# Softmax weights divided ahead of the turn, values as transposed rows, the mask on GpSimd, and logits over parts of the columns

## The reference

```python
def forgetting_attention(q, k, v, f, ...):          # 6 heads of 64, blocks of 128 query rows
    c = cumsum(log_sigmoid(f + f_bias))
    s = (q_block @ k[:hi].T) * scale + c[lo:hi, None] - c[None, :hi]
    s = where(k_pos <= q_pos, s, -inf)
    out = softmax(s) @ v[:hi]
def hybrid_mixer(h, ...):
    return concatenate([o_dn, o_fx, o_pl]) @ w_out    # gated DeltaNet 384, attention 384, pooling 256
def moe_swiglu(h, router, w_gate, w_up, w_down):      # 8 experts, 1536 wide, top 2
    probs = softmax(h @ router); gates = top 2 of probs, normalised
    out = sum over e of gates[:, e] * ((silu(h @ w_gate[e]) * (h @ w_up[e])) @ w_down[e])
```

## Time and profile before

| | |
|---|---|
| median of 3 runs | 1545.66 us (1545.61 to 1547.28) |
| profiled execution | 1552.2 us |
| span of its instructions | 1550.3 us |
| TensorE busy | 1518.6 us (98%) |
| VectorE busy | 1186.3 us (77%) |
| ScalarE busy | 1015.9 us (66%) |
| GpSimd busy | 70.1 us (5%) |
| mean granted TensorE clock | 0.993 of full |

### The profile page before, as it was taken

One profiled execution on the slowest core, in us unless ns is written; L12 is line 12 of the kernel. 1 busy time (PEld: TensorE's weight loads), 2 busy tenths in 40 slices (PEclk: granted clock), 3 DMA queues, 4 the chain that ended last, 5 costly groups with the idle time before them and its releaser, 6 DMA issues.

```text
span 1550.3 us, 27067 instructions
## 1 busy us (share of the span) xinstructions
PE 1518.6 (98%) x9990; PEld 1303.5 (84%) x9990; DVE 1186.3 (77%) x1485; ACT 1015.9 (66%) x1433; POOL 70.1 (5%) x92
## 2 busy tenths in 40 slices
PE   9999999999999999999999999999999999999998
PEld 7988888878878888899788888998788888888886
DVE  6677877775678877787776556886688888888887
ACT  6666656565566656696564445875467777777775
POOL 0000000000000000031000000120000000000000
PEclk9999999999999999999999999999899999999999
DMA  7544554544525555464154555461699999999995
GB/s 282 185 144 170 190 189 186 190 151 175 190 82 176 204 189 189 141 196 161 58 211 184 202 189 181 149 185 42 244 366 358 408 382 381 384 403 388 371 362 220
DMA packets 54795, 351.09 MB, mean 226 GB/s; under 512 B 6208, under 2 KB 9968, under 8 KB 14896
## 3 DMA queue, kind: packets, MB, share of 16 engines
q1 hardware_dynamic: 46512, 330.94, 57.2%
q0 software_dynamic: 8192, 18.90, 4.7%
HBM read 341.90 MB, written 7.91 MB: 226 GB/s over the span
## 4 chain that ended last, share of the span: by engine, by line
PE 90%; DVE 4%; ACT 3%; issue 1%; DMA 0%; POOL 0%; DVEq 0%; ACTq 0%; SPq 0%; POOLq 0%
PE PS L966 21%; PE PS L1920 16%; PE PS L2053 14%; PE PS L2089 11%; PE PS L1938 8%; PE PS L2054 8%; PE PS L1536 1%; DVE EWL L3850 1%; PE PS L2024 1%; PE PS L1901 1%; ACT MWH L2312 1%; DVE MWL L3174 1%; PE PS L1132 1%; PE PS L1038 1%; PE PS L2114 0%
## 5 line engine op out<-in xcount | busy, mean ns | idle before, releaser
L3850 DVE TENSOR_TENSOR EWL<-W,EWH 128x2048 fp32r<-128x2048 f32 x144 | 329.2, 2292 | 41.6 <-ACT EWH L2867 40.4
L2053 PE MATMUL PS<-HTB,WH 128*128 128x512 f32 x944 | 329.9, 393 | 0.0
L2867 ACT ACTIVATE EWH<-W 128x2048 fp32r<-128x2048 f32 x144 | 276.9, 1923 | 56.5 <-PE PS L1938 30.4
L2054 PE MATMUL PS<-HTB,WL 128*128 128x256 f32 x1008 | 282.5, 280 | 0.0
L3166 DVE TENSOR_TENSOR WL<-W,WH 128x2048 fp32r<-128x2048 f32 x99 | 226.5, 2288 | 35.2 <-ACT WH L2288 32.1
L2288 ACT ACTIVATE WH<-W 128x2048 fp32r<-128x2048 f32 x99 | 189.2, 1917 | 97.8 <-PE PS L2054 86.9
L966 PE MATMUL PS<-MWH,HTB 128*128 128x256 f32 (+1 forms) x940 | 240.5, 341 | 2.4 <-issue 1.5
L3174 DVE TENSOR_TENSOR MWL<-W,MWH 128x1024 fp32r<-128x1024 f32 x136 | 166.6, 1238 | 70.3 <-ACT MWH L2312 67.7
L2053 PEld LDWEIGHTS PS<-HTB,WH 128*128 128x128 f32 x944 | 177.2, 188 | 40.5
L2312 ACT ACTIVATE MWH<-W 128x1024 fp32r<-128x1024 f32 x136 | 142.3, 1055 | 83.2 <-PE PS L966 76.0
L2054 PEld LDWEIGHTS PS<-HTB,WL 128*128 128x128 f32 x1008 | 189.6, 188 | 1.0
(11 more groups left out here) (425 smaller groups left out, 2445.5 us busy)
## 6 DMA issues: line engine op xcount, KB each, us to landing
W<-in_weights SPq DMA_DIRECT2D x311, 1024.0 KB, 5.5
CS<-in_consts POOLq DMA_DIRECT2D x4, 403.5 KB, 4.8
ARENA<-rows_m POOLq DMA_DIRECT2D x8, 192.0 KB, 7.2
ARENA<-rows_m POOLq DMA_DIRECT2D x2, 768.0 KB, 12.5
moe_acc<-X POOLq DMA_DIRECT2D x3, 512.0 KB, 12.3
moe_rows<-HN POOLq DMA_DIRECT2D x3, 512.0 KB, 12.3
X<-in_x SPq DMA_DIRECT2D x2, 512.0 KB, 4.3
W<-in_weights SPq DMA_DIRECT2D x2, 512.0 KB, 6.3
```

Source lines behind the costliest of these rows:

```text
L2053: mm(PS[b][:, :], WH[:, sl, o:o + P], HTB[:, :, kk, :], start=(kk == 0), stop=False, skip_group_check=True)
L2054: ins = mm(PS[b][:, 0:256], WL[:, sl, o:o + P], HTH[:, kk, :], start=False, stop=(kk == KC - 1), skip_group_check=True)
L2867: A(EWH[tile % SPLIT][:, :], tile_ap(w0 + tile), ACT.Copy).then_inc(sem("moe_hi"), 1)
L3850: TT(EWL[tile % SPLIT][:, :], tile_ap(w0 + tile), EWH[tile % SPLIT][:, :].bitcast(F32), SUB).then_inc(sem("moe_lo"), 1)
```

## The change

- **Mask.** ScalarE's copy L2757 goes. GpSimd writes MB with two additions, mask plus row term, as soon as the bank of the turned rows is free, ahead of its accumulating DMAs.
- **Softmax.** One `tensor_tensor_reduce` per row tile adds scores and MB, negates, and reduces; ScalarE's exponential takes scale -1. The bank is given back after the reduction. The new `fx_divided(h)` on VectorE takes reciprocals and scales the exponentials, and `fx_turn` waits for it. `fx_turn(0)` comes after `fx_scores(1)`, and the banks are planned anew.
- **Values.** `fx_values` has FV as weights and PT moving, two heads in the two column halves, and so writes channels by rows. `fx_out` (ScalarE) and `fx_out_lo` (VectorE) write them to HTH and HTL. The division at the end and one of two groups of six transposes, with their splits, go. The output projection's chunk order becomes 6, 7, 3, 4, 5, 2, 0, 1, and `chunk_read(1, 1)` follows chunk 6.
- **Logits.** The router's matrix (padded to 32 columns) is the weight operand, in four column groups with HT moving; ScalarE copies the parts and two matmuls with a picking matrix add them up. Its preparation moves from the start of the kernel to the dilated mixer.
- **Router and start of the MoE.** `kept_at_work` issues matmuls whose result is not used, four ahead of the placing and one behind it. The last norm's scaling is split, so that the second tile's halves (`last_scaled`) lie beside the placing. The selection for experts 1 to 7 and `gates` come after the first gate product, `stage` is split around a weight tile, and `slots_turned` and `turn_selection(3)` move one group of columns later.

```diff
-M2_OUT_CHUNKS = (6, 7, 4, 5, 3, 2, 0, 1)
+M2_OUT_CHUNKS = (6, 7, 3, 4, 5, 2, 0, 1)
...
-            pool.wait_ge(sem(m + "_gd"), 3)
+            await_free_of(pool, (m, "rowT"))
+            for t, sl in enumerate((slice(0, P), slice(P, 384))):
+                w = sl.stop - sl.start
+                pool.tensor_tensor(m2.MB[:, :, sl], bc(cst("cmask")[:, sl], 1, 6), bc(st_gc[:, t, 1, :], 2, w), ADD).then_inc(sem("masks_written"), 1)
+            pool.wait_ge(sem("masks_written"), 2 if m == "m0" else 4)
...
+            def logit_parts():
+
+                key = ("router", "parts")
+                claim(pe, key)
+                for b in range(4):
+                    await_free_of(pe, ("norm", 7, b))
+                for r in range(2):
+                    for j in range(4):
+                        out = bank(key)[32 * j:32 * j + 32, 0:S]
+                        ins = mm(out, st_rt[:, 4 * r + j, :], HT[:, 4 * r + j, :], start=(r == 0), stop=(r == 1), skip_group_check=True)
+                done(ins, key)
+
+            def logits():
+
+                key = ("router", "logits")
+                claim(pe, key)
+                await_free_of(pe, ("router", "parts"))
+                for t in range(NT):
+                    ins = mm(bank(key)[:, t * 8:(t + 1) * 8], mo.PARTS[:, t * P:(t + 1) * P], st_pick, start=(t == 0), stop=(t == NT - 1),
+                             skip_group_check=True)
+                done(ins, key)
 
             turned(0)
             turned(1)
-            claim(pe, ("router", "logits"))
-            logits(0)
-            done(logits(1), ("router", "logits"))
+            logit_parts()
+            logits()
+
+        def kept_at_work(n):
+
+            for k in range(n):
+                mm(PS[3][:, 0:256], ident, X[:, 0, 0:256], start=True, stop=True, skip_group_check=True)
...
-                    pe.wait_ge(sem(m + "f_e"), h + 1)
+                    pe.wait_ge(sem("fx_divided"), 6 * l + h + 1)
...
             def fx_values(g):
 
-                for h in (2 * g, 2 * g + 1):
-                    await_free_of(pe, (m + "f", "t", h))
-                    for n in range(NT):
-                        key = (m + "f", "o", n)
-                        if h == 0:
-                            claim(pe, key)
-                        for kt in range(n + 1):
-                            b = n + kt
-                            ins = mm(bank(key)[:, h * 64:(h + 1) * 64], m2.PT[:, h % 2, b * P:(b + 1) * P], m2.FV[:, kt, h * 64:(h + 1) * 64],
-                                     start=(kt == 0), stop=(kt == n))
-                        if h == FX_H - 1:
-                            done(ins, key)
+                key = (m + "f", "o", g)
+                claim(pe, key)
+                for r in range(2):
+                    await_free_of(pe, (m + "f", "t", 2 * g + r))
+                for kt in range(NT):
+                    for r in range(2):
+                        h = 2 * g + r
+                        ins = mm(bank(key)[half[r], kt * P:256], m2.FV[:, kt, h * 64:(h + 1) * 64], m2.PT[:, h % 2, kt * 256:256 + kt * P],
+                                 start=(kt == 0), stop=(kt == NT - 1), skip_group_check=True)
+                done(ins, key)
...
-            fx_turn(0)
             pe.wait_ge(sem("m2_qd"), l + 1)
             state_out(1)
             fx_scores(1)
+            fx_turn(0)
...
-            for n in range(NT):
-                await_free_of(pe, (m + "f", "o", n))
+            await_free_of(pe, (m, "pz"))
+            await_free_of(pe, (m + "f", "o", 0))
+            await_free_of(pe, (m + "f", "o", 1))
+            m2_chunk(6, first=True)
+            chunk_read(1, 1)
+            m2_chunk(7)
+            m2_chunk(3)
+            m2_chunk(4)
+            for t in range(NT):
+                await_free_of(pe, (m, "o", t))
             for j in range(2):
                 transposed(m, j, M2_OT[j])
-            chunk_read(1, 1)
-            await_free_of(pe, (m, "pz"))
-            m2_chunk(6, first=True)
-            m2_chunk(7)
+            await_free_of(pe, (m + "f", "o", 2))
+            m2_chunk(5)
             for j in range(2):
-                await_free_of(pe, (m, "oT", j))
-            m2_chunk(4)
-            m2_chunk(5)
-            for t in range(NT):
-                await_free_of(pe, (m, "o", t))
-            for j in range(2, 4):
-                transposed(m, j, M2_OT[j])
-            m2_chunk(3)
-            for j in range(2, 4):
                 await_free_of(pe, (m, "oT", j))
             m2_chunk(2)
...
+            kept_at_work(4)
...
-                pe.wait_ge(sem("hn"), 2 * NT * 8)
                 for c in range(KC):
+                    if c % 4 == 0:
+                        pe.wait_ge(sem("hn"), 2 * NT * 8 - (0 if c else 1))
...
-                if not p and gs == 0:
+                if not p and gs == 1:

...
+            release(A(mo.PARTS, bank(key)[:, 0:S], ACT.Copy), key)
...
-                        ins = A(m2.EX[:, h % 2, sl], m2.SM[:, h % 2, sl], ACT.Exp, bias=st_mx[:, j:j + 1], accum_out=st_sum[:, j:j + 1])
+                        ins = A(m2.EX[:, h % 2, sl], m2.SM[:, h % 2, sl], ACT.Exp, scale=-1.0, bias=st_mx[:, j:j + 1], accum_out=st_sum[:, j:j + 1])
...
+            def fx_out(g):
+
+                key = (m + "f", "o", g)
+                await_full(act, key)
+                out_hi(A(HTH[:, 3 + g, :], bank(key)[:, 0:256], ACT.Copy))
...
-            A(m2.MB, bc(cst("cmask"), 1, 6), ACT.Copy).then_inc(sem(m + "_gd"), 1)
...
+            TT(st_rt[:, :, 0:N_EXP], v3(prm("router"), KC), bc(prm("norm")[:, 7 * KC:8 * KC], 2, N_EXP), MUL)
+            dve.tensor_reduce(st_pick, ident.rearrange("p (j e) -> p e j", j=4)[:, 0:N_EXP, :], AX.X, ADD)
...
-                    ins = STT(m2.SM[:, h % 2, sl], bank(key)[:, sl], st_gc[:, n, 1, h:h + 1], m2.MB[:, h, sl], ADD, ADD)
-                release(ins, key)
-                await_free_of(dve, key)
+                    ins = dve.tensor_tensor_reduce(m2.SM[:, h % 2, sl], bank(key)[:, sl], m2.MB[:, h, sl], -1.0, -NEG, ADD, MIN,
+                                                   st_mx[:, 2 * h + n:2 * h + n + 1])
+                ins.then_inc(sem(m + "f_mx"), 1)
+                dve.wait_ge(sem(m + "f_mx"), h + 1)
+                dve.sem_inc(free[uses[key][0]], 1)
+
+            def fx_divided(h):
+
+                dve.wait_ge(sem(m + "f_e"), h + 1)
+                link(dve.reciprocal(st_ri[:, 2 * h:2 * h + 2], st_sum[:, 2 * h:2 * h + 2]))
                 for n, sl in enumerate((slice(0, P), slice(P, 384))):
-                    ins = dve.tensor_reduce(st_mx[:, 2 * h + n:2 * h + n + 1], m2.SM[:, h % 2, sl], AX.X, MAX, negate=True)
-                ins.then_inc(sem(m + "f_mx"), 1)
+                    at = m2.EX[:, h % 2, sl]
+                    ins = TS(at, at, st_ri[:, 2 * h + n:2 * h + n + 1], None, MUL)
+                ins.then_inc(sem("fx_divided"), 1)
+
+            def fx_out_lo(g):
+
+                key = (m + "f", "o", g)
+                await_out_hi()
+                release(TT(HTL[:, 3 + g, :], bank(key)[:, 0:256], HTH[:, 3 + g, :].bitcast(F32), SUB), key)
...
+            last_scaled(1, 0)
             key = ("router", "place")
             await_full(dve, key)
             link(TT(mo.POS, mo.POS, bank(key)[:, 0:16], ADD))
             select(mo.SEL, slice(0, 1))
+            last_scaled(1, 1)
             link(dve.tensor_reduce(mo.MOST, bank(key)[:, 16:24], AX.X, MAX))
             release(TS(MORE[0:1, :], mo.MOST[0:1, :], P + 0.5, None, ALU.is_gt), key)
             await_free_of(dve, key)
             dve.sem_inc(sem("more"), 1)
-            select(mo.SEL, slice(1, N_EXP))
...
+                if not p and gs == 0:
+                    select(mo.SEL, slice(1, N_EXP))
+                    gates()
```

More of the change, by code:

```diff
@@ L428, in plan_m2 @@
         pair("w")
-        for n in range(NT):
-            plan((m + "f", "o", n), 2 + n)
+        for g in range(2):
+            plan((m + "f", "o", g), 2 + g)
         for t in range(NT):
@@ L446, in plan_m2 @@
         rot((m, "vp", 3))
+        rot((m + "f", "o", 2))
         rot = Rot([6, 7])
-        for j in range(4):
+        for j in range(2):
             rot((m, "oT", j))
@@ L501, in build @@
         elif st[0] == "router":
+            plan(("router", "parts"), 6)
             plan(("router", "logits"), 4)
@@ L2280, in hi @@
                 if prev_mixer[name] != "od":
[L2281 removed]
+                    await_full(act, (prev_mixer[name], "oT", 3 if prev_mixer[name] == "ev" else len(M2_OT) - 1))
                 elif j == 0:
@@ L2827, in mixer2 @@
             out_square(0)
+            fx_out(0)
             fx_exp(2)
+            fx_out(1)
             fx_turned(2)
-            for j in range(2):
-                m2_out_T(m, j)
+            fx_out(2)
+            out_root(0)
             out_square(1)
-            out_root(0)
             fd(27)
@@ L3111, in last_norm, with last_scaled @@
             dve.wait_ge(s_late, 16 * (LATE + 1))
```

(25 more changed lines are left out.)

44 lines of the change are left out of this document (19 added, 25 removed).

## The result

Seven executions of the changed kernel took 1551.72 us in the median (1550.32 to 1554.51), seven of the kernel before 1546.79 (1545.61 to 1547.58). The ratio is 1.0033, with a 95% interval from 1.0023 to 1.0043: slower by some 5 us, where 1543.8 had been forecast. The profiled executions say the opposite: 1550.32 us after, 1552.2 before. Which of the two is right, and why they differ, is the first thing to settle.

What follows compares the result with a forecast made beforehand. TensorE, busy 1518.6 of 1550.3 us, was taken as the bound. Mask +7.4, attention -3.2, router -1.8 and second mixer's clock -4.25 sum to -1.85 us on the median 1545.66: 1543.8 us, range 1535.5 to 1552.5.

Steps and rivals of the forecast that it cites:

- part 4: Second mixer's attention: its half-clock stretch disappears as waits go and work gets denser; 4.25 us gained.
- part 2: Attention: less TensorE work and old waits gone, against a new wait for the division; 1.6 us gained per mixer, 3.2 both.
- part 3: Router and MoE start: TensorE 3.4 us earlier at its first expert, but VectorE sets the pace; 1.8 us gained.
- part 1: Mask on GpSimd: its additions hold VectorE, TensorE stalls before the first 64x64 products; 3.7 us lost per mixer, 7.4 both.
- the sum's last sentence: Whole kernel: -1.85 us applied to the median 1545.66, the profile's extra 6.5 us taken as the profiler's own; 1543.8 us.
- The rival on the clock: Both mixers: each gets a half-clock stretch of 4.25 us, 1552.3 us in all, or 1548.1 with one; chance 0.25.
- the prediction's signs of being wrong: No idle at the first 64x64 products, a new half-clock stretch behind them, or attention's TensorE waits above 4 us.

Runs made afterwards that it cites:

- e2: Kernel before with the mask alone moved from ScalarE to two GpSimd additions; 1553.13 us, ratio 1.0038.
- e4: Kernel before with the attention's parts of the change alone, mask on ScalarE; 1546.51 us, ratio 0.9995.
- e6: e1 with three unused matmuls on TensorE ahead of the third turn of the softmax weights; 1542.59 us, ratio 0.9972.
- e9: e1 with the last pair of heads brought forward on VectorE and ScalarE, no unused matmuls in the attention; 1540.54 us, ratio 0.9965.
- e3: Kernel before with the router and the start of the experts changed alone; 1545.67 us, ratio 0.9992.
- e8: Kernel before with ScalarE's mask copy removed and two GpSimd memsets in place of the additions, causal mask left out; 1546.38 us, ratio 0.9993.
- e7: e1 without the five unused matmuls of the router; 1547.68 us, ratio 1.0006.
- e5: Changed kernel with five unused matmuls on TensorE in the stall before the first 64x64 products, both mixers; 1550.95 us, ratio 1.0025.
- e1: Changed kernel with the mask copied by ScalarE again, nothing of it on GpSimd, row term left out; 1544.76 us, ratio 0.9988.

## Why the prediction was wrong

The sum missed the median by 7.9 us, of which part 4 is 4.25, part 2 is 3.2 and part 3 is 0.95, with 0.8 the other way from part 1: 7.6 together.

- **The failing step is part 4, the clock of the second mixer (-4.25 us), and the sum's last sentence.** The stretch was read from one execution of 1552.2 us, and the 6.5 us between it and the median were put down to the profiler. The profiler costs nothing that these runs show: executions of the changed kernel at a clock of 0.997 agree (1550.32 profiled, 1550.63 another). The difference was mostly this stretch (4.25). By their mean clock 26 of 29 executions of the kernel before lack it. Measured, the term is 0 against the median. Without it the sum is +2.4, 1548.1 us: slower, and not faster.
- **Part 1, the mask: right in mechanism, price 6.6 (e2) for 7.4.** The wait was 2.1 us and not 3.7: the additions took 4.39 us together for the 5.3 forecast, VectorE's first operation was hardly held, and the second lost 2.56 us to an addition of 2.94, where 0.56 + 3.47 had been taken. The half-clock stretch behind the stall, 1.8 us a mixer, was put into a rival and not into the sum; that the two errors nearly cancel is luck.
- **Part 2, the attention, fails as well: 0.0 (e4) for -3.2.** The work came out better than the value taken (0.87 us a group, for 1.1). The new wait of 1.4 us was in the sum at its size, and its consequence, the clock, was not: e4's clocks were 0.994 to 0.995 in the middle, where before 0.996 to 0.997, and with the wait filled or gone (e6, e9) 2.2 and 4.2 us came back. By TensorE's order the changed kernel gained 1.1 us in each mixer's attention in the profiled run, without a stretch; with one, nothing is left.
- **Part 3, the router: -0.85 (e3) for -1.8.** VectorE sets the pace there, as forecast (1.47 us waited before L1962, where no such wait was). The profiled pair shows 2.26 us, the best case: the profile of before had a half-clock stretch in the router 3.4 us longer, so 1.7 us dearer, than those of e2 and e4 (e8's was as long as it), and the changed kernel's profile was one of two without the stretch ahead of the first down projection. The part forecast the clock at 1.00 through the router, and put nothing for the clock behind the waits for VectorE that it foresaw there.
- **The rival on the clock** had the right sign, and part of the mechanism: a stretch did follow each stall in the profile, which was one of the prediction's signs of being wrong. That its 1552.3 lies by the median of 1551.72 is luck. It charged 8.5 us for two stretches that cost 1.8 each, and kept the 4.25 of part 4 and the 3.2 of part 2, which were not there.

The sum by parts with the measured terms is +5.75 us, against +4.9 measured. What remains open: what decides, between one execution and the next, whether a wait of 1.4 us, or the stall of 2.1, brings the clock down; the same code was seen with and without.

## What to carry to other kernels

Before a term of a sum is read from a profile, look whether the profiled execution is like the others: its mean clock and time against those of the plain runs say so at once, and a clock stretch that only one has is no gain. Price a wait on TensorE twice, once by its length and once by the half clock that may follow it; where it cannot be taken away by an order that brings its producer forward (e9), unused matmuls in it can be worth their place (2.2 us in e6, 2.9 in e7, only 0.8 in e5). Moving work to an engine that looks idle was not free here, because it read SBUF while operations of VectorE on the critical path read two tiles of it: 4.4 us of GpSimd's time cost 3.3 us of the kernel's, twice.

## What the runs showed of the hardware

- A wait of 1.4 us on TensorE, in a part that was less than fully busy around it, went with a fall to 1.2 GHz in some executions (e1 and e4, for 3.4 to 6.8 us) and not in others (the changed kernel's profile); filled with work, most executions had a mean clock of 0.999 (six of eight).
- A stall of 2.1 us was followed by 3.4 us at 1.2 GHz in three of four cases (both mixers of the changed kernel, the first of e2) and by none in the second mixer of e2.
- A VectorE operation on two SBUF tiles of 128x256, begun 0.24 us after a GpSimd addition of 2.94 us, took 2.98 us instead of 0.42; beside GpSimd memsets the pair kept its 0.76.
- Matmuls of 32 columns of weights in four column groups: 16 records of 256 columns in 1.07 us, 0.26 ns a column pass, where one after another it would be 0.82.
- The sum-and-maximum operation of VectorE on 128x128 and 128x256, one input in PSUM, took 0.29 and 0.42 us, each with a 0.08 us read of its accumulator.
